# Attention of a two-layer diffusion trunk: the second exponential of a 768-key pair in two parts, and the inverse row sums turned by one transpose

## The reference, cut to what matters

```python
# A: every latent query sees 512 latent and 256 context keys
s = jnp.einsum('bqhgd,bkhd->bhgqk', q, k).astype(F32) * (q.shape[-1] ** -0.5)
p = jax.nn.softmax(s, axis=-1).astype(v.dtype)
o = jnp.einsum('bhgqk,bkhd->bqhgd', p, v)
...
# B: a window of latent keys with a learned bias, and the 256 context keys
p = jax.nn.softmax(jnp.concatenate([s_loc, s_ctx], axis=-1), axis=-1).astype(v.dtype)
```

## The kernel before

| engine | iteration p |
|---|---|
| TensorE | scores p; PV p-2; inverse sums p-2; transposes p-1 |
| VectorE | (bias and) maximum p, both heads; reciprocal p-1; `o` p-2; probT copy p-1 |
| ScalarE, A | exponential p, heads 0 and 1; inverse copy p-2; probT copies p-1 |
| ScalarE, B | exponential p, head 0; inverse copy p-2; probT copy p-1; exponential p, head 1 |

## Time and profile before

### The profile page before, as it was taken

The page is one execution under the profiler, slowest core; times in us unless marked ns, Lnnn a source line. Parts: engine busy times, 40 slices in busy tenths (PEclk is TensorE's granted clock), DMA queues, the critical chain, the costliest instruction groups (busy, mean ns, idle before and its releaser), DMA issues. The chain is left out here.

```text
span 2981.0 us, 57501 instructions
## 1 busy us (share of the span) xinstructions
PE 2845.9 (95%) x24887; PEld 2450.6 (82%) x24887; DVE 1147.6 (38%) x1791; ACT 1056.0 (35%) x1803; POOL 1046.7 (35%) x721
## 2 busy tenths in 40 slices
PE   6999999988999999999999999899999999999999
PEld 5878888866799988899999877788777788878887
DVE  3854432355711123422222377434235622242223
ACT  4543332245622223322222265433226532343223
POOL 3334543302133332222222233455321344434443
PEclk8999999999999999999999999999999999999999
DMA  7215322200022221222212131422210034323332
GB/s 257 62 30 195 127 73 73 60 19 9 4 66 65 88 88 57 68 66 65 64 59 65 55 99 43 144 88 69 76 43 4 24 96 138 106 85 92 99 99 78
DMA packets 306026, 230.88 MB, mean 77 GB/s; under 512 B 25264, under 2 KB 277616, under 8 KB 304880
## 3 DMA queue, kind: packets, MB, share of 16 engines
q1 hardware_dynamic: 299152, 202.48, 22.6%
q0 software_dynamic: 3776, 17.91, 1.7%
q10 hardware_dynamic: 2848, 6.82, 0.6%
HBM read 216.17 MB, written 11.98 MB: 77 GB/s over the span
## 5 line engine op out<-in xcount | busy, mean ns | idle before, releaser
L2265 POOL TENSOR_TENSOR wl<-wring,wh 128x1024 fp32r<-128x1024 f32 (+1 forms) x310 | 721.1, 2328 | 1332.3 <-ACT wh L1340 1327.9
L486 PE MATMUL ps<-hh,wh 128*128 128x496 f32 (+2 forms) x2168 | 769.1, 355 | 6.9 <-DVE R L2112 3.5
L488 PE MATMUL ps<-hh,wl 128*128 128x496 f32 (+2 forms) x2168 | 758.5, 350 | 0.0
L487 PE MATMUL ps<-hl,wh 128*128 128x496 f32 (+2 forms) x2168 | 758.5, 350 | 0.0
L1340 ACT ACTIVATE wh<-wring 128x1024 fp32r<-128x1024 f32 (+1 forms) x310 | 306.0, 988 | 445.7 <-PE ps L488 422.5
L486 PEld LDWEIGHTS ps<-hh,wh 128*128 128x128 f32 x2168 | 409.0, 189 | 65.1 <-issue 6.1
L487 PEld LDWEIGHTS ps<-hl,wh 128*128 128x128 f32 x2168 | 409.2, 189 | 52.2 <-issue 3.4
L488 PEld LDWEIGHTS ps<-hh,wl 128*128 128x128 f32 x2168 | 408.7, 189 | 49.7
L488 PE MATMUL ps<-fh,wl 128*128 128x496 f32 (+2 forms) x744 | 262.8, 353 | 0.0
L487 PE MATMUL ps<-fl,wh 128*128 128x496 f32 (+2 forms) x744 | 262.8, 353 | 0.0
L486 PE MATMUL ps<-fh,wh 128*128 128x496 f32 (+2 forms) x744 | 262.8, 353 | 0.0
(11 more groups left out here) (322 smaller groups left out, 4271.7 us busy)
## 6 DMA issues: line engine op xcount, KB each, us to landing
wring<-in_w_ffn SPq DMA_DIRECT2D x128, 512.0 KB, 3.6
wring<-in_w_in SPq DMA_DIRECT2D x110, 512.0 KB, 3.6
wboth<-in_w_mod SPq DMA_DIRECT2D x80, 512.0 KB, 5.4
wring<-in_w_branch SPq DMA_DIRECT2D x32, 256.0 KB, 2.6
wring<-in_w_out SPq DMA_DIRECT2D x16, 512.0 KB, 4.1
x_store<-R POOLq DMA_DIRECT2D x2, 3072.0 KB, 9.1
R<-x_store POOLq DMA_DIRECT2D x2, 3072.0 KB, 11.1
wring<-in_w_in SPq DMA_DIRECT2D x16, 256.0 KB, 4.0
```

The lines of the kernel that those rows point to most:

```text
L486: mm(ps[:, t0:t1], ahk, rh[:, k, t0:t1], start=(k == 0), stop=False)
L487: mm(ps[:, t0:t1], ahk, rl[:, k, t0:t1], start=False, stop=False)
L488: last = mm(ps[:, t0:t1], alk, rh[:, k, t0:t1], start=False, stop=(k == kn - 1))
L2265: G.tensor_tensor(slot_view(wl, n % NSPL, l, name, i), w, slot_view(wh, n % NSPL, l, name, i).bitcast(F32), ALU.subtract)\
```

## The change

Four edits, all in the attention of both layers.

1. For latent pairs of branch A the second head's exponential is issued as two, first the 256 context columns (marked "exp context"), then the 512 latent columns (marked "exp"). Each has a row sum of its own; the second goes to a column of `small`, and VectorE adds the two with a 128x1 addition and waits for its result.
2. TensorE issues the context scores of a branch A pair first and lets them wait only for "exp context" of the pair before; the latent scores wait for "exp" of the last latent pair. Context tiles of A now take their scores in the context columns of PS[0] and PS[1].
3. The reciprocal is written 128 wide to `invs`, a view of 128 columns of `gex`: each head's inverse 64 times. TensorE turns it with a single 128x128 transpose where it had two matmuls. This holds for both branches.
4. On VectorE the reciprocal, with the addition, stands behind the product `o` of the pair before instead of ahead of it.

```diff
--- before.py
+++ after.py
@@ -224,6 +224,7 @@
         prow = sb("prow", [P, P])
         mrow = sb("mrow", [P, P])
         orec = mrow
+        invs = gex[:, 0:4, :, :].rearrange("p t h n -> p (t h n)")
         tiles = ([4, 5, 0, 1, 2, 3], [5, 4, 3, 2, 1, 0])
         masks = {k: cst[:, C_TRI + HALF * n:C_TRI + HALF * n + HALF] for n, k in enumerate(("UI", "LI", "US", "LS"))}
         ident_half = cst[:, C_IDH:C_IDH + HALF]
@@ -353,7 +354,20 @@
 
         def score_ps(l, p):
 
-            return (PS[0], PS[1]) if att_pairs(l)[p][0] == "A" else (PS[p % 2][:, 0:512], PS[p % 2][:, 512:1024])
+            br, _, t = att_pairs(l)[p]
+            if br == "A":
+                return (PS[0], PS[1]) if t < LT else (PS[0][:, LAT:], PS[1][:, LAT:])
+            return PS[p % 2][:, 0:512], PS[p % 2][:, 512:1024]
+
+        def in_parts(l, p):
+
+            br, _, t = att_pairs(l)[p]
+            return br == "A" and t < LT
+
+        def last_latents(l, p):
+
+            t = att_pairs(l)[p][2]
+            return p - 1 if t else p - 1 - (TT - LT if l == 0 else 0)
 
         def windowed(v):
 
@@ -581,17 +595,21 @@
                             pe.wait_ge(*read("vbs", l, 3))
                         back = 1 if br == "A" or work[p - 1][0] == "A" else 2
                         if p:
-                            pe.wait_ge(*act_done.at("exp", l, p - back, 1))
+                            pe.wait_ge(*act_done.at("exp context" if br == "A" and in_parts(l, p - 1) else "exp",
+                                                    l, p - back, 1))
                         ps = score_ps(l, p)
                         ctx = (LAT, TOK)
                         if t >= LT:
                             runs = ((0, ctx),)
                         elif br == "A":
-                            runs = ((0, (0, LAT)), (LAT, ctx))
+                            runs = ((LAT, ctx), (0, (0, LAT)))
                         else:
                             w0 = (0, 64, 192, 256)[t]
                             runs = ((0, (w0, w0 + 256)), (256, ctx))
                         for c0, (n0, n1) in runs:
+                            if br == "A" and n0 == 0 and p:
+
+                                pe.wait_ge(*act_done.at("exp", l, last_latents(l, p), 1))
                             for u in range(2):
                                 lo = HD * u
                                 q, k = (qk[:, hp, :], qk[:, 4, :]) if br == "A" else (qB[:, hp, :], kB[:, hp, :])
@@ -619,11 +637,7 @@
                                 mm(PS[3][HD * u:HD * u + HD, 512:512 + P], vt[b][:, c0:c0 + HD],
                                    probT[br][:, u, b, :], start=(b == 0), stop=(b == nk - 1))
                         pe.wait_ge(*dve_done.at("rsum", l, p - 2))
-                        for u in range(2):
-                            inv = stat[:, 2 * ((p - 2) % 4) + u, 1:2]
-                            last = mm(PS[3][HD * u:HD * u + HD, 512 + P:512 + 2 * P], inv.to_broadcast([P, HD]), ident,
-                                      start=True, stop=True)
-                        last.then_inc(*pe_done.mark("O", l, p - 2))
+                        tr(PS[3][:, 512 + P:512 + 2 * P], invs, ident).then_inc(*pe_done.mark("O", l, p - 2))
                     if 1 <= p <= len(work):
 
                         br, hp, t = work[p - 1]
@@ -1136,6 +1150,13 @@
                 if p == len(work) // 2 + 1:
                     eng.wait_ge(*pe_done.at("O", l, p - 2))
                 sl = 2 * (p % 4) + u
+                if u and in_parts(l, p):
+                    for key, c0, c1, total in (("exp context", LAT, n, stat[:, sl, 1:2]),
+                                               ("exp", 0, LAT, small[:, 57 + p % 2:58 + p % 2])):
+                        nc.scalar.activation(prob[br][p % 2][:, u, c0:c1], score_ps(l, p)[u][:, c0:c1], ACT.Exp,
+                                             bias=stat[:, sl, 0:1], accum_out=total)\
+                            .then_inc(*act_done.mark(key, l, p, u))
+                    return
                 nc.scalar.activation(prob[br][p % 2][:, u, 0:n], score_ps(l, p)[u][:, 0:n], ACT.Exp,
                                      bias=stat[:, sl, 0:1], accum_out=stat[:, sl, 1:2])\
                     .then_inc(*act_done.mark("exp", l, p, u))
@@ -1821,10 +1842,6 @@
                                 dve.wait_ge(*dve_done.at("bias", l, p, u))
                             V.tensor_reduce(stat[:, sl, 0:1], ps[:, 0:n], AX.X, ALU.max, negate=True)\
                                 .then_inc(*dve_done.mark("max", l, p, u))
-                    if 1 <= p <= len(work):
-                        sums = stat[:, 2 * ((p - 1) % 4):2 * ((p - 1) % 4) + 2, 1:2]
-                        dve.wait_ge(*act_done.at("exp", l, p - 1, 1))
-                        V.reciprocal(sums, sums).then_inc(*dve_done.mark("rsum", l, p - 1))
                     if p >= 2:
                         br, hp, t = work[p - 2]
                         dve.wait_ge(*act_done.at("rsums", l, p - 2))
@@ -1834,6 +1851,16 @@
                             o = by_window(oB[:, hp, 0:LAT])[:, 2 * t:2 * t + 2, :, :]
                             ps, inv = (v.rearrange("p (g r c) -> p g r c", g=2, r=8) for v in (ps, inv))
                         V.tensor_tensor(o, ps, inv, ALU.mult).then_inc(*dve_done.mark("o", l, p - 2))
+                    if 1 <= p <= len(work):
+                        sums = stat[:, 2 * ((p - 1) % 4):2 * ((p - 1) % 4) + 2, 1:2]
+                        dve.wait_ge(*act_done.at("exp", l, p - 1, 1))
+                        if in_parts(l, p - 1):
+                            part = small[:, 57 + (p - 1) % 2:58 + (p - 1) % 2]
+                            V.tensor_tensor(sums[:, 1, :], sums[:, 1, :], part, ALU.add)\
+                                .then_inc(*dve_done.mark("sum", l, p - 1))
+                            dve.wait_ge(*dve_done.at("sum", l, p - 1))
+                        V.reciprocal(invs.rearrange("p (u e) -> p u e", u=2), sums.to_broadcast([P, 2, HD]))\
+                            .then_inc(*dve_done.mark("rsum", l, p - 1))
                     if 1 <= p <= len(work):
                         br, hp, t = work[p - 1]
                         nb = min(key_tiles(br, t), 4)
```

## The result

The changed kernel takes 3018.4 us (median of 4 runs, 3012.1 to 3020.1) against 2982.2 before (4 runs, 2979.1 to 2986.0). The ratio is 1.011, with a 95% interval of 1.0091 to 1.0128: 1.1% slower, clear of noise, on the forecast's side and at its number. The profiled run is the fastest of the four, 3012.1 us with a span of 3010.2, so its trace has to explain 29 us, not 36.

The account below looks back on a forecast made before the run. TensorE orders branch A's 4.63 us steps and VectorE nearly fills branch B's 3.33 us; 9.2 + 7.1 + 12.2 + 8.3 = 36.8 us on 2982.8 gives 3019.6, less 1.4 for the median 3018; range 3004 to 3034.

Parts of the forecast that it names:

- The wide reciprocal: On VectorE, 128 outputs per partition take 954 ns and hold the engine 0.87 us, against 0.155 us for 2 before.
- rival A: The reciprocal costs by its two distinct values, so TensorE's 4.48 us decides; about 2979 us, not slower; chance 0.05.
- Its place: VectorE, reciprocal behind o and ahead of the probT copy: delays that copy, the next pair's maxima and PV; 0.87 us.
- The step sizes: Steady latent steps: branch A, 768 keys, 4.63 to 5.20 us; branch B, 512 keys, 3.33 to 3.82 us.
- The groups of six: Layer 0, four latent and two context steps: branch A 25.66 us plus 2.6, branch B 18.71 plus 2.83.
- The split costs, the early scores give nothing: Branch A: split exponential +0.26 us, addition +0.20; early scores gain 0.15 us in each of a layer's first two steps.
- The transpose: TensorE, one transpose for two matmuls: 0.15 us less, worth nothing in steps that VectorE bounds.
- The sum: Attention of both layers, branches A and B: 9.2 and 12.2 us in layer 0, 7.1 and 8.3 in layer 1.
- The first two steps of layer 0: Branch A, where nothing stands behind o: the early context scores gain an estimated 0.15 us in each.
- Its tail: Branch B, last pairs of the layer, where the probT copy lies bare: 0.9 us more.
- Rival B, the clock: TensorE's clock falls once in each of layer 0's eight groups, at least 1.4 us each: 11 us, 3029; chance 0.08.
- Rival C: The copy's waits for the transposes hide much of the reciprocal: half the loss, about 18 us, 3000; chance 0.04.

Follow-up runs that it names:

- experiments 1 and 2: Against the changed kernel: first, 2-wide reciprocal and two matmuls put back, 2984.4 us; second, 2-wide reciprocal plus 128-wide copy instead of the 128-wide reciprocal, 2993.1 us.
- experiment 3: Changed kernel with the second exponential whole again and scores in their old order; 128-wide reciprocal behind o and one transpose stay: 3009.6 us.
- experiment 5: Changed kernel with the addition and 128-wide reciprocal moved back ahead of o, two buffers taking turns: 2992.3 us.
- experiment 6: Kernel before plus only the exponential in two parts and the early context scores; 2-wide reciprocal and two matmuls in their old place: 2985.0 us.
- wide_A_early: Kernel before with, in branch A alone, the 128-wide reciprocal ahead of o (two buffers) and one transpose; no split: 2986.7 us.
- experiment 7: Three other orders against the kernel before, to keep the gain of one transpose in branch A: 2986.7, 2988.5 and 2983.5 us.
- experiment 4: The changed kernel unaltered, run again for a second profile: 3022.0 us, ratio 1.0125 against the kernel before; its profiled run took 3023.0.

## Why the prediction was right, point by point

- **The wide reciprocal** was the main term and is shown: 954 ns was foreseen from another stage's row, 947 measured, and experiments 1 and 2 isolate it. It holds VectorE 0.87 us (642.42 to 643.29), as forecast. That its 128 values come from two repeated ones makes it no cheaper; this disposes of rival A. The loss is not its alone, though: in branch A most of it needs the split as well (experiment 3). The forecast's sum has that, since it adds both on one way and takes the longer of this and TensorE's; without split and addition it gives 5.21 - 0.46 = 4.75, the mean of experiment 3's steps.
- **Its place.** The forecast said that it delays the copy, the next maxima and PV. The timeline has all three, and experiment 5 takes the delay away in branch A by moving it back.
- **The step sizes** were 5.20 and 3.82; measured 5.09 to 5.10, and 3.77. One term is half of the difference in A and all of it in B: I let the probT copy hold VectorE 0.60 us, and behind the long reciprocal it held it 0.54. In branch A the maximum also led to the exponential 0.97 later instead of 1.00, and the two parts of the exponential together took 0.03 less.
- **The groups of six**: forecast 28.26 (25.66 + 2.6) and 21.54; measured 28.03 and 21.52. That B agrees to 0.02 is luck: its latent steps (783.68 to 798.47) rose by 2.44, where I had 2.66, and its context steps by 0.37, where I had 0.17. In A (651.91 to 671.86) it is 2.39 against 2.77, and 0.02 less against 0.17 less.
- **The split costs, the early scores give nothing.** Right in kind: experiment 3 gains by undoing them and experiment 6 shows them neutral by themselves. The price was 0.46 for a step; 0.35 is what undoing them brings.
- **The transpose** was mis-sized: I had 0.15 us less for TensorE, and it is 0.10. In wide_A_early, where TensorE's loads follow each other as before, it takes 3.04 us from PV's first load to the next scores' (2289.84 to 2292.88) and 3.14 before (2296.53 to 2299.67). Up to the transposes 0.16 is saved, and 0.06 is lost again until the scores. That is the difference between the 4.53 of experiment 7 and the 4.48 that I worked with. The transpose is worth something only where TensorE orders the step, and in the changed kernel's steady steps it does not.
- **The sum** was 36.8 for the four parts, and they measured 31.4 and 32.6: it was 4 to 5 us too large. The smaller steps are half of it. The first two steps of layer 0 gained 1.06 us, where I had 0.3: from the first scores to the third it is 9.36 (622.42 to 631.78), 10.42 before. The second scores start 0.43 sooner and are 0.20 shorter, the third another 0.43 sooner. From maximum to maximum the two steps gained 0.82, and in layer 1 1.52 (2248.05 to 2256.96, 10.43 before); where the clock falls in them differs from profile to profile. And layer 1's branch B had a stretch at the lower clock before and none after (granted clock 0.97 and 1.00): its first two steps took 10.2 us after 11.5, from scores to scores. Its tail went the other way, +1.4 where I had 0.9. The median moved 36 all the same. That it agrees with 3018 to 0.4 us is luck: the terms don't earn it. The difference of some 4 us is not in the attention parts as profiled, and outside them single profiles differ by 10. It doesn't hang on the wide reciprocal: in every experiment, those without it too, the median moved 0.5 to 7 us more than the parts of its profile, and all of them are measured against one profile of before. Part of it goes with the clock (experiment 4). Whether the change has any part in it isn't settled.
- **Rival B, the clock**, fell: 1.00 in steady windows with TensorE busy 3.73 of 5.09 us, and over the four parts 0.97 to 1.00 in the first profile and 0.95 to 1.00 in the second, where it was 0.96 to 0.98 before. The Trainium skill's statement (TensorE: Matmul & The Clock Gate, the part on PE-mode transpose), that transposes don't count as activity in the same way, did not show here: steps with 13 transposes in them ran at 1.00. But other matmuls stand between them, and no run separates the two.
- **Rival C** fell too: the copy starts right behind the reciprocal, and all its waits together went from 6.2 us to 0.0.

## What to carry to other kernels

Count an instruction's outputs before widening it, and look for its price in the row of the same operation at that width, in whatever stage it stands: here one row from a norm gave the answer before the change was built. Then ask what stands behind it in its engine's queue: in branch A the same 0.87 us was free ahead of `o` and cost 0.5 us a step behind it, together with the split. And if one edit makes an engine late, the edits that shorten another engine's way lose their worth, or turn into cost.

## What the runs showed of the hardware

- VectorE's reciprocal took 155 ns for 2 outputs for each partition and 947 for 128, or 6.3 ns for each more; a copy to the same 128 places took 230 to 250 ns in all. Reading each of two values 64 times instead of 128 values made the reciprocal no cheaper (947 against 954 ns).
- An instruction right behind the long reciprocal was shorter: the 128x512 copy 628 ns instead of 683, and `o` 0.23 us instead of 0.27 in experiment 5's branch B. With a 2-wide reciprocal or a 128-wide copy ahead of it, the 128x512 copy was not (680 and 683).
- Two parts of an exponential, 256 and 512 columns, each with its own row sum, hold ScalarE for 0.45 and 0.66 us to the next start, against 0.88 in one piece, so the split costs it 0.23 us.
